# Layer 1's mixing: adding up the blocks of later keys and the position bias on VectorE instead of in TensorE's accumulation

## What is computed

```python
z = (jnp.einsum('bqhd,bshd->bhqs', q, k) * (q.shape[-1] ** -0.5)
     + offset.astype(jnp.float32)[None, :, None, None])
mask = (k_pos[None, :] < q_pos[:, None])[None, None]
log_beta = jax.nn.log_sigmoid(z)
log_rest = jnp.where(mask, jax.nn.log_sigmoid(-z), 0.0)
between = lax.cumsum(log_rest, axis=3, reverse=True) - log_rest
weight = jnp.where(mask, jnp.exp(log_beta + between), 0.0)
return jnp.einsum('bhqs,bshd->bqhd', weight, v)
...
mixed = jnp.einsum('gts,bnsgc->bntgc', w, vc) + jnp.transpose(b_s[:, :L])[None, None, :, :, None]
return u * mixed.reshape(B, T, G, c)
```

## Time and profile before

| | |
|---|---|
| median of 3 runs | 2369.11 us (2363.33 to 2373.26) |
| the profiled execution | 2370.67 us, its span 2369.1 us |
| TensorE matmul busy | 2222.4 us, 94% of the span |
| VectorE busy | 1158.1 us, 49% |
| ScalarE busy | 599.2 us, 25% |
| chain of work that ended last | PE 78%, DVE 10%, DMA 4%, ACT 4%, issue 3% |

### The profile page before, as it was taken

The page is one execution under the profiler, slowest core; times in us unless marked ns, Lnnn a source line. Parts: engine busy times, 40 slices in busy tenths (PEclk is TensorE's granted clock), DMA queues, the critical chain, the costliest instruction groups (busy, mean ns, idle before and its releaser), DMA issues.

```text
span 2369.1 us, 45894 instructions
## 1 busy us (share of the span) xinstructions
PE 2222.4 (94%) x17191; PEld 1963.2 (83%) x17191; DVE 1158.1 (49%) x3560; ACT 599.2 (25%) x741; POOL 189.7 (8%) x301
## 2 busy tenths in 40 slices
PE   6789999999999999989979997999999999999997
PEld 2168888888888889889978897888888788898997
DVE  1533333423334333454353266777777677745332
ACT  1312122221212121132233233232223223223221
POOL 0000100101010101100000001111011111100111
PEclk9989998999999999999989999999999999999999
DMA  9976554455645455434342246788878878953442
GB/s 317 316 209 210 163 160 148 149 164 157 187 145 176 131 179 170 127 91 119 113 150 72 72 137 211 261 267 275 285 248 269 273 249 269 301 167 112 129 132 63
DMA packets 399998, 436.68 MB, mean 184 GB/s; under 512 B 16916, under 2 KB 306990, under 8 KB 399167
## 3 DMA queue, kind: packets, MB, share of 16 engines
q1 hardware_dynamic: 359270, 311.99, 42.9%
q0 software_dynamic: 30752, 113.67, 14.0%
q10 hardware_dynamic: 9810, 8.73, 1.1%
HBM read 407.79 MB, written 26.54 MB: 183 GB/s over the span
## 4 chain that ended last, share of the span: by engine, by line
PE 78%; DVE 10%; DMA 4%; ACT 4%; issue 3%; SPq 0%; POOL 0%; DVEq 0%; ACTq 0%; POOLq 0%
PE pt L535 59%; PE m L535 17%; DVE arena L1708 3%; ACT w_hi L962 2%; PE m L539 2%; ACT arena L962 1%; DMA arena<-in_cache_k 1%; DMA raw<-in_e_w_ada 1%; DVE w_lo L1334 1%; DMA arena<-in_o_k_norm_g 1%; PE pt L539 0%; DVE arena L1872 0%; DVE act_lo L1414 0%; DVE arena L1453 0%; DVE arena L1762 0%
## 5 line engine op out<-in xcount | busy, mean ns | idle before, releaser
L535 PE MATMUL pt<-act_hi,w_hi 128*128 128x260 f32 x4384 | 919.7, 292 | 39.2 <-DVE w_lo L1334 13.1
L535 PE MATMUL pt<-act_lo,w_hi 128*128 128x260 f32 x4384 | 895.8, 287 | 1.6 <-issue 1.6
L535 PE MATMUL pt<-act_hi,w_lo 128*128 128x260 f32 x4384 | 895.6, 286 | 0.0
L1334 DVE TENSOR_TENSOR w_lo<-raw,w_hi 128x1024 fp32r<-128x1024 f32 x274 | 335.4, 1224 | 925.1 <-ACT w_hi L962 924.3
L535 PEld LDWEIGHTS pt<-act_hi,w_hi 128*128 128x128 f32 x4384 | 690.4, 193 | 110.2 <-issue 92.8
L535 PEld LDWEIGHTS pt<-act_lo,w_hi 128*128 128x128 f32 x4384 | 691.1, 193 | 1.7 <-issue 1.7
L535 PEld LDWEIGHTS pt<-act_hi,w_lo 128*128 128x128 f32 x4384 | 689.8, 192 | 0.0
L962 ACT ACTIVATE w_hi<-raw 128x1024 fp32r<-128x1024 f32 x274 | 289.9, 1058 | 1197.8 <-PE pt L535 1181.6
L1708 DVE CUSTOM_DVE_ANT_0 arena<-arena 128x128 f32<-128x128 f32 x1024 | 224.1, 288 | 41.7 <-DMA arena<-in_cache_k 41.3
L962 ACT ACTIVATE arena<-arena 128x1040 f32<-128x1040 f32 (+8 forms) x199 | 170.1, 863 | 237.4 <-DVE arena L1808 77.9
L535 PE MATMUL m<-arena 128*128 128x128 f32 (+7 forms) x1136 | 201.1, 338 | 2.9 <-DVE arena L1560 1.6
(11 more groups left out here) (161 smaller groups left out, 1092.2 us busy)
## 6 DMA issues: line engine op xcount, KB each, us to landing
arena<-in_cache_k POOLq DMA_DIRECT2D x128, 512.0 KB, 5.0
arena<-in_cache_v SPq DMA_DIRECT2D x128, 512.0 KB, 5.0
raw<-in_o_w_in SPq DMA_DIRECT2D x112, 512.0 KB, 5.6
raw<-in_e_w_in SPq DMA_DIRECT2D x98, 512.0 KB, 4.2
raw<-in_e_w_ada SPq DMA_DIRECT2D x96, 512.0 KB, 5.7
raw<-in_o_w_ada SPq DMA_DIRECT2D x96, 512.0 KB, 5.0
raw<-in_e_w_out SPq DMA_DIRECT2D x32, 512.0 KB, 3.9
raw<-in_o_w_out SPq DMA_DIRECT2D x32, 512.0 KB, 4.7
```

Of the source, the lines that this page charges most:

```text
L535: return pe.matmul(out, lhsT, rhs, start=start, stop=stop, skip_group_check=True)
L1334: tt(w_lo[:, b, :], raw[:, sl, :], w_hi[:, b, :].bitcast(F32), ALU.subtract)\
```

## The change

- **between**: VectorE first adds the blocks' columns into `above`, a piece of `tmp[1]` (which held the queries and is free after z): block 2 and block 3 for the queries of block 3 (used for key block 1), the same plus block 1 (for key block 0), and block 1 plus block 2 for the queries of block 2. These are three adds of 128x128 behind the four masks, with two waits of VectorE for itself, and `rest` is given behind the last. The `ones` matmuls then go over disjoint columns: 768 columns in five matmuls instead of 1280 in six.
- **oc**: the four single-row bias matmuls are gone. The bias of the head is loaded to all 128 partitions of `brow`, and `gate` adds it: one add of 512 columns from `M[1]` into `tmp[3]`, a wait for itself, and then the multiplication that was there, now from `tmp[3]`.
- The bias transfer leaves its place behind `ws` and stands behind page 3, where GpSimd waits for `gated` of the head before (its last reader) and for the query row. It counts on `qb`, the semaphore of the query row; so the query row waits for the bias before it, and `gate` for its own bias. `ws_in` counts one transfer for a head instead of two.

```diff
@@ TensorE
-                pe.wait_ge(s("ws_in"), i * 32 + 32)
+                pe.wait_ge(s("ws_in"), i * 16 + 16)
...
-                    for l in range(b + 1, NT):
-                        last = mm(m012[:, off + P * (l - b):off + T - P * b], ones[:, :],
-                                  za[:, SB_OFF[l]:SB_OFF[l] + T - P * l], start=False, stop=(l == 3))
+                    for at, x in (((P, za[:, 512:640]), (2 * P, above[:, 128:384])),
+                                  ((P, za[:, 1024:1152]), (2 * P, above[:, 0:128])), ((P, za[:, 896:1024]),), ())[b]:
+                        last = mm(m012[:, off + at:off + at + x.shape[1]], ones[:, :], x, start=False, stop=True)
...
-                    mm(M[1][:, P * t:P * t + P], vntok[:, t, :], wst, start=True, stop=False)
-                    last = mm(M[1][:, P * t:P * t + P], ones[0:1, :], brow[0:1, 0:P], start=False, stop=True)
+                    last = mm(M[1][:, P * t:P * t + P], vntok[:, t, :], wst)
@@ VectorE, gate(n)
-                tt(to[:, 0:T], G[4][:, 0:T], M[1], ALU.mult)
+                dve.wait_ge(s("qb"), 32 * HC if isinstance(n, int) and n == HC else n * 32 + 16)
+                step(tt(tmp[3][:, 0:T].rearrange("p (t k) -> p t k", t=NT), M[1].rearrange("p (t k) -> p t k", t=NT),
+                        brow[:, 0:P].unsqueeze(1).to_broadcast([P, NT, P]), ALU.add))
+                tt(to[:, 0:T], G[4][:, 0:T], tmp[3][:, 0:T], ALU.mult)
@@ VectorE, mix1
-                masks(za).then_inc(s("rest"), 1)
+                step(masks(za))
+                tt(above[:, 128:256], za[:, 640:768], za[:, 1024:1152], ALU.add)
+                step(tt(above[:, 0:128], za[:, 1152:1280], za[:, 896:1024], ALU.add))
+                tt(above[:, 256:384], za[:, 768:896], above[:, 0:128], ALU.add).then_inc(s("rest"), 1)
@@ GpSimd
-                pool.dma_start(brow[0:1, 0:P], a["o_b_s"][0, bass.ds(h, 1)]).then_inc(s("ws_in"), 16)
+            def head_bias(h):
+                if not (isinstance(h, int) and h == 0):
+                    pool.wait_ge(s("gated"), h)
...
+                if not (isinstance(h, int) and h == HC - 1):
+                    pool.wait_ge(s("qb"), h * 32 + 32)
...
+                pool.dma_start(brow[:, 0:P], a["o_b_s"][0, bass.ds(h, 1), :].rearrange("b n -> (b n)")
+                               .partition_broadcast(P)).then_inc(s("qb"), 16)
```

More of the change, by code:

```diff
@@ L216, in build @@
         orow = z[:, 0:256]
+        above = tmp[1][:, 0:384]
         eps = sb("eps", [P, 1])
@@ L1702, in key_page @@
                 if p == 0:
-                    dve.wait_ge(s("qb"), b * 16 + 16)
+                    dve.wait_ge(s("qb"), 16 if isinstance(b, int) and b == 0 else b * 32)
                 slot = key_slot(p)
@@ L1892, in _ @@
             with dve.Fori(0, 3) as n:
-                step.body(n, 0, 24)
+                step.body(n, 0, 30)
                 l1b(n * 2 + 1, 1)
                 l1b(n * 2 + 2, 0)
-            step.end(3, 24)
+            step.end(3, 30)
             l1b(7, 1, True)
@@ L1968, in head_weights @@
                 pool.dma_start(ws, a["o_w_s"][0, bass.ds(h, 1)].rearrange("g t s -> t (g s)")).then_inc(s("ws_in"), 16)
-                pool.dma_start(brow[0:1, 0:P], a["o_b_s"][0, bass.ds(h, 1)]).then_inc(s("ws_in"), 16)
+            def head_bias(h):
+                if not (isinstance(h, int) and h == 0):
+                    pool.wait_ge(s("gated"), h)
+                    pool.sem_inc(s("pool_waited"), 1)
+                if not (isinstance(h, int) and h == HC - 1):
+                    pool.wait_ge(s("qb"), h * 32 + 32)
+                    pool.sem_inc(s("pool_waited"), 1)
+                pool.dma_start(brow[:, 0:P], a["o_b_s"][0, bass.ds(h, 1), :].rearrange("b n -> (b n)")
+                               .partition_broadcast(P)).then_inc(s("qb"), 16)
             def sample_keys(b):
@@ L1976, in sample_keys @@
                             pool.wait_ge(s("q_out"), 16)
+                        if not (isinstance(b, int) and b < 2):
+                            pool.wait_ge(s("qb"), b * 32 - 16)
+                            pool.sem_inc(s("pool_waited"), 1)
                         queries(b)
@@ L1979, in sample_keys @@
                             head_weights(b - 1)
+                    if p == 3 and not (isinstance(b, int) and b == 0):
+                        head_bias(b - 1)
             sample_keys(0)
@@ L1985, in layer1_pages @@
             head_weights(HC - 1)
+            pool.wait_ge(s("qb"), 32 * HC - 16)
+            head_bias(HC - 1)
         @block.gpsimd
```

## The result

| | before | after |
|---|---|---|
| median of the runs taken side by side | 2368.24 us (2362.44 to 2375.32, 7 runs) | 2390.28 us (2379.72 to 2395.85, 7 runs) |
| profiled execution | 2370.67 us | 2395.85 us |
| chain: PE, DVE, DMA, issue | 78, 10, 4, 3% | 65, 16, 9, 5% |

The ratio is 1.0092, with a 95% interval from 1.0068 to 1.0116. The change makes the kernel 22 us slower; the forecast was 2365 us with a range up to 2376. The profiled execution of after is the slowest of its seven, 5.6 us above their median.

The account below looks back on a forecast made before the run. TensorE and VectorE run nearly level, each head as long as the slower path. Gains of 1.7 us (heads 1 to 6) and 3.0 (head 7), less 0.7 at the output projection, make 4.0: 2365 us, range 2352 to 2376.

Parts of the forecast that it names:

- oc saves: TensorE in oc: four of eight matmuls go, the rest fall to 0.22 us each; 2.45 us a head less.
- the rival in which its matmuls stay at 0.416 us: In oc: the remaining matmuls keep their pace, 1.66 us a head goes, 2366 us; chance 0.05.
- Between saves: TensorE in between: 512 columns of ones matmuls less, 0.86 us a head.
- The three adds: VectorE behind the masks, ahead of between: 0.84 us more, ends 0.61 and 1.0.
- The wait at the samples' sum: After unit 1, TensorE would newly wait for line 1823, up to 1.6 us.
- Head 7: The head without key pages: 2.1 us gained at the samples' sum and 0.86 in between, 3.0 us.
- Page 4: GpSimd's queue, behind its wait for gated: hidden; if the order turned, a late page, at most 1 to 2 us a head.
- Gate's add: VectorE in gate: one add of 512 columns out of PSUM, 0.72 us with its wait, ends 0.60 and 0.75.
- VectorE's way from line 1823 to z: Gate and six key pages: 6.0 us of waits less 6 x 0.72 for gate, z 1.7 us earlier over heads 1 to 6.
- the room at the samples' sum: TensorE comes 0.9 to 2.1 us after line 1823 ends; at most 12.2 of oc's 17.2 us pass in heads 1 to 7.
- the clock: Rival: clock falls behind TensorE's longer waits ahead of between; all six heads cost 9.6 us, 2375 us; chance 0.17.

Follow-up runs that it names:

- the first hold: Changed kernel with value page 5, and what stands behind it in SyncE's queue, issued only after key page 5 of the next head landed: 2383.86 us, ratio 1.0076.
- the four useless single-row matmuls: Changed kernel with four single-row matmuls of 128 columns put back into oc, into PSUM columns that nothing reads: 2370.26 us, ratio 1.0018.
- half value pages: Only 512 of 1024 columns of each value page loaded: kernel before 2364.69 us, ratio 0.9974; changed kernel 2357.40 us, ratio 0.9956.
- eleven matmuls: Changed kernel with eleven full-height matmuls of 128 columns behind oc's own, into PSUM columns that nothing reads: ratio 1.0035, median 2383.46 us.

## Why the prediction was wrong

**Right.** oc saves 5.49 - 3.08 = 2.41 us against 2.45, and the rival in which its matmuls stay at 0.416 us fell. Between saves 0.85 against 0.86. The three adds take 1805.36 - 1804.50 = 0.86 us against 0.84, and between starts 0.05 us behind the last. The wait at the samples' sum came, in heads 1, 2, 4, 6 and 7, at most 0.7 us. Head 7 gained 2.75 us against 3.0. Page 4 was not held by the bias's transfer: in head 3 that was issued at 1764.57, page 4 at 1768.27, when page 2 was reduced. Gate's add was 0.83 us, above the upper end of 0.75.

**The step that failed** is "VectorE's way from line 1823 to z", where a page was taken to land in 5.2 us as before. That number was a median over 96 pages; the two that VectorE waits for ahead of z went from means of 5.2 and 5.6 us (pages 5 and 7) to 7.4 and 6.9, 3.5 us a head. The way from the end of line 1823 to VectorE's z, forecast to become 1.7 us shorter over heads 1 to 6, became 15.1 us longer (222.1 instead of 207.0), of which gate's add is 5.0; against TensorE's z, VectorE came 24.1 us later. The argument counted the room at the samples' sum (0.9 to 2.1 us a head, 12.2 in seven heads, 10.1 in heads 1 to 6) as free time that TensorE could take. TensorE did take 9.1 us, counted at the matmul that waits (the prediction read the room against the sum's first matmul, which doesn't wait and starts 0.22 us sooner). But this room was the lead by which key page 5 was issued ahead of TensorE's value pages. The queues' share of 0.82 in a clean stretch stood in the earlier trace rows, and head 4 showed the price of a short lead: 1.10 us of lead there at the sum, 3.91 us of wait. I read it as a page that happened to be late.

**The rival that came nearest** was the clock. Its 9.6 us are six times 6.19 - 4.60 = 1.6 us, by which between was longer in head 4 of before, at a granted clock of 0.50, than in head 3. Its sign came, windows at 0.50 behind between, and its price was near: six falls of the clock cost 12.2 us against the 9.6 of the prediction. That sum took all six as new although head 4's was there already; five new ones at 1.6 us would have been 8.0, and measured were 12.2 - 1.6 = 10.6 us more. Its condition was set by waits of 2 to 3 us; they were 4.7 to 6.5, and all six fell. The granted clock was 0.50 behind each of these waits, and 1.00 in the first 3 us of between in all six heads once twenty matmuls filled them. The length of the wait alone does not tell, though: in other runs the clock fell behind waits of 2.0 and 2.2 us and did not behind 3.1 and 3.3 (last section).

So of 24.8 us in heads 1 to 6, the clock behind the waits ahead of between is 10.6, and late pages and the waits for line 1768, less what TensorE gained, the rest. Over the whole of these heads the clock cost less: it no longer falls behind oc. TensorE was busy in 15.8 us of halved stretches before and in 31.8 after, which at about half pace is an estimated 8 us more. That TensorE's pace decides is shown by taking work out of it alone and by giving the pace back, and the part of the transfers by halving the value pages and by the first hold, which brought VectorE to z in time; that a 512 KB page issued together with others is held up by them is read from the landing times (key page 5 of head 3: 4.7 us when issued 2.07 us ahead of value page 5, 7.2 us when issued 0.25 us behind it) and was not measured by itself.

## What to carry to other kernels

Room of one engine ahead of a meeting point may be the lead of its transfers over those of another engine. Before you shorten the engine that waits least, list per stage which transfers it triggers, what is in flight at that moment, and how full the queues are (here 0.8); a median landing time hides the one page that counts. If removing work makes a kernel slower, put the same time back as useless work: a kernel that recovers tells that the pace, and not what the work did, is the cause. Landing times before and after, and a lighter or a held transfer, then tell whether the transfers are what the pace acts on.

## What the runs showed of the hardware

- Of the 512 KB key pages 5 of heads 1 to 6, in before those issued 1.3 us or more ahead of the value page landed in 4.5 to 5.4 us; in before and after, those issued from 0.5 us ahead to 0.9 us behind it in 6.3 to 8.0. It is no sharp rule: with the four useless single-row matmuls, pages issued 1.4 us ahead landed in 5.4, 5.6 and 6.3 us.
- A full float32 matmul of 128 columns takes 0.22 us, and 0.416 with single-row ones between the earlier trace rows; in the changed kernel, without these, the granted clock did not fall right behind oc in heads 0 to 6, where in before it was 0.50 behind oc of heads 1, 2, 4 and 6.
- The clock behind a wait ahead of between, by case: 0.50 from at most 0.3 us behind between's start where the wait was 4.7 to 6.5 us (after, six heads), and also from 1.0 us behind it where it was 2.2 us (half value pages, head 5) and from 1.2 us where it was 1.95 us (eleven matmuls, head 6); 1.00 behind 3.3 us (half value pages, head 1) and 3.1 us (four single rows, head 6).
- TensorE's wait at the loop's back edge was at most 3.5 us in before, 1.6 in the changed kernel, 3.9 with four matmuls more in oc, and 5.6 and 6.0 with eleven and with five full ones. It ended each time 1.7 to 1.9 us behind the landing of a 16 KB transfer of the kind `instruction`. I had not expected added instructions to cost anything there.
